# A down projection with four groups of block products done as seven products of sums

## The chip, the cores and the metric

The kernel runs on one core of one Trainium2 chip. Its engines work side by side and meet at semaphores: TensorE (PE in the profile, its weight loads PEld) multiplies, VectorE (DVE) and ScalarE (ACT) work element by element, GpSimd (POOL) does a few small steps, and SyncE (SP) issues nearly all transfers between HBM and on-chip memory (SBUF). TensorE writes to PSUM. The metric is the time of one execution in microseconds on the device, the median of several runs.

## What is computed

Two transformer blocks over 256 tokens of width 2048, in f32. The part that changes is the feed-forward step at the end of the first block:

```python
u = jnp.square(jax.nn.relu(jnp.einsum('bsd,df->bsf', h, w_up[l])))
x = x + rms_norm(jnp.einsum('bsf,fd->bsd', u, w_down[l]), norm_mlp_post[l])
```

`u` is 256 x 8192 and `w_down` 8192 x 2048. Ahead of it stand the first block's attention and the up projection, behind it the whole second block (its input projection `w_in_2` comes next) and the output.

## The kernel before

All large products run over a list of chunks. A chunk is 512 rows and up to 512 columns of a weight matrix, 1 MB; the program has 342, numbered in the order in which TensorE takes them. The down projection has chunks 176 to 239: four blocks of 512 output columns (`dn` 0 to 3), each 16 chunks deep. TensorE multiplies a chunk for both halves of the tokens (t = 0 and 1, 128 tokens each): per half 4 row tiles times 3 matmuls, so 24 matmuls of 128 x 512, summed in two banks of the PSUM tensor `acc`. The second PSUM tensor, `mis`, has four banks for side work.

Three matmuls take the place of one because every f32 operand is split into a high part and a rest, and high x high, high x rest and rest x high are added. The splits are the work around TensorE:

- A weight chunk is loaded by SyncE into one of `NRAW` = 3 buffers (`raw`, L398). ScalarE copies it into the high part (`high`, L578, tile `hi`), then VectorE subtracts (`low`, L994, tile `lo`). There are `NSPL` = 3 buffers for hi and lo, so the hi of a chunk waits for the product three chunks earlier; it is made two chunks ahead of its own product (`LEAD` = 2). A raw buffer is loaded again once the lo of its chunk is done.
- The operand from `u` is split the same way in pieces of 128 x 1024 (4 row tiles, both token halves) by `cut` (ScalarE L628, VectorE L1043), three chunks ahead, into one of four slots of `at`. Each of the four column blocks cuts all 16 pieces again, 64 cuts in all.

Each engine has its own queue and works it in order. A step n of the loops on ScalarE, VectorE and SyncE issues what belongs beside product n: the split of chunk n + 2, the cut for chunk n + 3, and side work named in a table (`beside`). `u` itself comes out of the up projection with tokens on partitions; it is turned block by block by VectorE and through HBM, one store and four loads for each of 16 pieces (`turned`); the last of these runs beside the first chunks of the down projection.

At the end of a column block ScalarE squares and copies the result out of PSUM (`evac`) to `Y2`; VectorE multiplies it with the norm's weights (`weigh`, steps 228 to 230 for the first three blocks). The change of stage to the next projection is written out by hand (`turnover`): TensorE does the first token half of the last three chunks, then the second half of two of them, so that the row mean, the norm and the transposes of the new rows for t = 0 run beside it; the first three chunks of the next stage are split early into `spare` buffers.

```python
def products(n, t):
    ...
    if n > 2:
        pe.wait_ge(s_lo, "lo", n)
    if source == "u":
        pe.wait_ge(s_dve, "cut", i)
    ...
        mm(o, a, hv[:, j, :], k + j == 0, False)
        mm(o, a, lv[:, j, :], False, False)
        r = mm(o, c, hv[:, j, :], False, k + j == nk - 1)
```

Of the kernel before, what the change touches and what calls it, by code (L numbers as in the profile page):

```python
# [15 lines left out]
P = 128  # L16
D = 2048
S = 256
# [3 lines left out]
NRAW = 3  # L22
# [4 lines left out]
N_W, N_AB, N_WO, N_UP, N_DN, N_IN2, N_RES, N_PG, N_ALL = 0, 80, 96, 112, 176, 240, 308, 326, 342  # L27
EARLY = {N_UP: (100, 101, 102), N_IN2: (231, 233, 237)}
# [41 lines left out]
def program(nc, x, xt, w_in, w_a, w_b, w_out, w_up, w_down, w_in2, w_out2, w_pg, w_pe, p2,  # L70
            cols, lamv, rpb, rows, bif, cos_c, sin_c, nam_c, id_c, lvl_c, caus_c, out):
    with ExitStack() as ctx:
# [82 lines left out]
        Y2 = t2(64, 2048)  # L155
        JK2 = SM[:, 0:512]
# [60 lines left out]
        for j in range(16):  # L217
            plan("up", j, w_up, 0, 16, 512 * j, 512, "r1")
        for j in range(4):
            plan("dn", j, w_down, 0, 64, 512 * j, 512, "u")  # L220
# [17 lines left out]
        on_dve = ("rope", "a", "b", "wo", "z", "g", "res")  # L238
# [5 lines left out]
        def freed(b):  # L244

            kind, j = blocks[b][:2]
            return s_dve if kind in on_dve or (kind, j) == ("dn", 3) else s_act
# [13 lines left out]
        nth = {c: i for i, c in enumerate(order)}  # L261
# [17 lines left out]

        side = {}  # L280
# [5 lines left out]
        turns_of.update({("hf", 0): 244, ("hf", 1): 248, ("qk", 0): 252, ("qk", 1): 256, ("hq", 0): 264, ("hq", 1): 268})  # L286
# [21 lines left out]
        for j in range(2):
            beside(272 + 4 * j, "turn_v", j)
        beside(266, "hg", 0, 0)  # L310
        for i, n in enumerate((268, 269, 271)):
            beside(n, "gate", i)
        for i in range(1, 13):
            beside(270 + i, "hg", 0, i)
        for i in range(13):
            beside(283 + i, "hg", 1, i)
        beside(295, "ml_logs", 0)
        for h in range(6):
            beside(296 + h, "ml", h)
        for g in range(2):  # L320
            beside(302, "ya", g)
        beside(316, "p_parts")
# [66 lines left out]
        def sync(e):  # L389
# [5 lines left out]
            def raw(n):  # L395
                if nth[n] >= NRAW:
                    sp.wait_ge(s_lo, "lo", order[nth[n] - NRAW])
                e.dma_start(raw_of(n).rearrange("p (k c) -> p k c", c=chunks[n][0].shape[-1]), chunks[n][0]).then_inc(  # L398
                    s_raw[nth[n] % NRAW].on("raw", n), 16)

# [23 lines left out]
            for n in order[8:]:  # L424
# [63 lines left out]
                if n == 231:  # L488
                    sp.wait_ge(s_dve, "cut", 49)
                    load(NB, rows[0:1, 2048:4096].squeeze(0).partition_broadcast(P), "nb2")  # L490
                if n == 260:
                    sp.wait_ge(s_dve, "cut", 63)
                    load(REV, id_c[1], "turn")
                if n == 309:
# [3 lines left out]
                if n == 313:  # L498
# [3 lines left out]
                raw(n)  # L502
# [7 lines left out]
        def gpsimd(e):  # L510
# [15 lines left out]
            for n in range(N_ALL):  # L526
# [17 lines left out]
                if n in (N_WO + 15, N_DN + 63):  # L544
# [6 lines left out]
                if n == 274:  # L551
# [9 lines left out]
        def scalar(e):  # L561
# [8 lines left out]
            def high(n):  # L570
# [4 lines left out]
                if N_IN2 <= n < N_IN2 + 3:  # L575
                    ac.wait_ge(s_dve, "cut", (53, 57, 63)[n - N_IN2])
# [46 lines left out]
            def cut(i):  # L623
                if i >= 64:
                    return
                ac.wait_ge(loaded("heads", ("ut", i % 16)), "heads", ("ut", i % 16))
                ac.wait_ge(s_prod, "products", N_DN + i - 4, 1)
                e.activation(ATH[:, 4 * (i % 4):4 * (i % 4) + 4, :], UT[:, 4 * (i % 16):4 * (i % 16) + 4, :], ACT.Copy).then_inc(  # L628
                    s_ach.on("cut hi", i))
# [140 lines left out]
            def square(b, t):  # L770
                ac.wait_ge(s_prod, "products", blocks[b][3][-1], t)
# [1183 lines left out]
```

## Time and profile before

| | |
|---|---|
| median of 3 runs | 1935.83 us (1935.59 to 1936.46) |
| profiled execution, first to last instruction | 1933.5 us |
| TensorE busy | 1922.0 us, 99% |
| VectorE busy | 1250.8 us, 65% |
| ScalarE busy | 983.0 us, 51% |
| transfers | 415 MB, 215 GB/s on average |

The profile shows one execution. "Busy" is the time in which an engine had an instruction at work; matmuls overlap, so their single durations add up to more than the busy time. In lists of groups, `out<-in` names the tiles; a matmul `acc<-hi,at` multiplies the high part of weights with the activations in `at`. An arrow `<-` in brackets names what ended the idle time before an instruction. A line number is that of the kernel's text, often that of a helper: L1589 is every matmul, L976 every `tensor_tensor` issued through `tt`.

### The profile page before, as it was taken

How to read it: one execution, taken by the hardware profiler on the slowest of the kernel's cores; microseconds unless marked ns; L12 is line 12 of the kernel's file. 1: busy time of each engine (PE TensorE's matmuls, PEld its weight loads, DVE VectorE, ACT ScalarE, POOL GpSimd, SP SyncE). 2: the span in 40 equal slices, each digit the busy share in tenths (PEclk: the TensorE clock that was granted, in tenths of full speed). 3: DMA queues.
4: the chain of work that ended last, by engine and by line, in shares of the span. 5: the costliest groups of instructions: out<-in, count | busy, mean ns of one | idle time of the engine just before them, and what ended most of it. 6: DMA issues, size and time to landing. Idle time of an engine off the chain costs nothing.

```text
span 1933.5 us, 21919 instructions
## 1 busy us (share of the span) xinstructions
PE 1922.0 (99%) x8770; PEld 1601.5 (83%) x8770; DVE 1250.8 (65%) x1255; ACT 983.0 (51%) x951; POOL 17.8 (1%) x31
## 2 busy tenths in 40 slices
PE   9999999999999999999999999999999999999998
PEld 7888888888888888888888888888889888888886
DVE  7747658845666644445466666677587869676655
ACT  6334445646445444444455555555555546544543
POOL 0000000000000000000000000000000000000000
PEclk9999999999999999999999999999999999999999
DMA  9876977765777388888886555565687544556753
GB/s 323 251 231 174 267 257 216 233 246 196 241 228 255 112 241 246 239 240 243 244 248 204 192 191 189 193 231 181 188 222 253 185 164 156 176 174 224 231 203 109
DMA packets 386151, 415.48 MB, mean 215 GB/s; under 512 B 192509, under 2 KB 205057, under 8 KB 385409
## 3 DMA queue, kind: packets, MB, share of 16 engines
q1 hardware_dynamic: 385032, 412.49, 68.6%
q10 hardware_dynamic: 1016, 1.59, 0.2%
q8 instruction: 69, 1.13, 0.2%
q14 instruction: 34, 0.27, 0.0%
HBM read 388.86 MB, written 25.17 MB: 214 GB/s over the span
## 4 chain that ended last, share of the span: by engine, by line
PE 95%; DVE 2%; ACT 1%; issue 1%; POOL 0%; POOLq 0%; DVEq 0%; ACTq 0%
PE acc L1589 92%; PE mis L1589 3%; ACT hi L578 1%; DVE lo L994 1%; DVE m L976 1%; PE mis L1592 1%; ACT m L567 0%; DVE m L984 0%; DVE at L1036 0%; ACT at L617 0%; DVE m L1294 0%; ACT xs L567 0%; DVE xs L976 0%; DVE sm L984 0%; POOLq L1892 0%
## 5 line engine op out<-in xcount | busy, mean ns | idle before, releaser
L1589 PE MATMUL acc<-hi,at 128*128 128x512 f32 (+1 forms) x5344 | 1650.6, 388 | 0.3 <-DVE lo L994 0.3
L1589 PEld LDWEIGHTS acc<-hi,at 128*128 128x128 f32 x5344 | 1000.4, 188 | 201.7 <-DVE lo L994 1.2
L994 DVE TENSOR_TENSOR lo<-raw,hi 128x2048 fp32r<-128x2048 f32 (+1 forms) x333 | 752.9, 2264 | 529.6 <-ACT hi L578 529.3
L1589 PE MATMUL acc<-lo,at 128*128 128x512 f32 (+1 forms) x2672 | 1032.5, 387 | 0.0
L578 ACT ACTIVATE hi<-raw 128x2048 fp32r<-128x2048 f32 (+1 forms) x333 | 628.4, 1891 | 522.0 <-PE acc L1589 476.7
L1589 PEld LDWEIGHTS acc<-lo,at 128*128 128x128 f32 x2672 | 501.8, 188 | 98.6
L567 ACT ACTIVATE m<-acc,st 128x512 f32<-128x512 f32 (+2 forms) x104 | 69.6, 669 | 86.3 <-PE acc L1589 85.2
L976 DVE TENSOR_TENSOR m<-m 128x256 f32<-128x256 f32 (+1 forms) x145 | 75.1, 518 | 20.9 <-ACT m L567 16.4
L567 ACT ACTIVATE m<-m 128x512 f32<-128x512 f32 (+4 forms) x71 | 58.2, 819 | 53.2 <-DVE m L976 37.9
L1043 DVE TENSOR_TENSOR at<-m,at 128x1024 fp32r<-128x1024 f32 x64 | 78.0, 1219 | 2.8 <-ACT at L628 2.8
L628 ACT ACTIVATE at<-m 128x1024 fp32r<-128x1024 f32 x64 | 66.6, 1041 | 7.5 <-PE acc L1589 7.5
L617 ACT ACTIVATE at<-m 128x512 fp32r<-128x512 f32 x40 | 25.1, 631 | 65.3 <-DVE m L976 51.1
L1589 PE MATMUL mis<-m 128*128 128x128 f32 (+3 forms) x316 | 53.0, 312 | 0.4 <-DVE m L976 0.4
L1589 PEld LDWEIGHTS mis<-m 128*128 128x128 f32 x316 | 45.7, 190 | 7.5 <-DVE m L976 1.7
L1126 DVE STREAM_TRANSPOSE m<-m 128x512 f32<-128x512 f32 x50 | 35.5, 709 | 2.9
L1036 DVE TENSOR_TENSOR at<-m,at 128x512 fp32r<-128x512 f32 x40 | 27.4, 688 | 13.0 <-ACT at L617 12.6
L1589 PE MATMUL acc<-spare,at 128*128 128x512 f32 x144 | 34.7, 394 | 0.0
L1589 PEld LDWEIGHTS acc<-spare,at 128*128 128x128 f32 x144 | 26.6, 188 | 5.4
L516 POOL TENSOR_TENSOR st<-st,mhalf 128x1 f32<-128x1 f32 (+3 forms) x20 | 14.9, 746 | 1703.1 <-DVE st L980 1617.9
L567 ACT ACT_TABLE_LOAD x20 | 25.7, 1283 | 3.2 <-issue 2.6
L568 ACT ACTIVATE m<-m,st 128x256 f32<-128x256 f32 x16 | 8.2, 510 | 37.1 <-DVE st L980 37.1
L568 ACT ACTIVATE sm<-xs 128x512 f32<-128x512 f32 (+1 forms) x18 | 10.5, 585 | 25.3 <-DVE xs L976 25.2
(134 smaller groups left out, 529.9 us busy)
## 6 DMA issues: line engine op xcount, KB each, us to landing
raw<-in_w_in SPq DMA_DIRECT2D x133, 1024.0 KB, 5.3
raw<-in_w_up SPq DMA_DIRECT2D x64, 1024.0 KB, 6.4
raw<-in_w_down SPq DMA_DIRECT2D x64, 1024.0 KB, 5.1
raw<-in_w_out SPq DMA_DIRECT2D x32, 1024.0 KB, 5.2
m<-turned SPq DMA_DIRECT2D x144, 128.0 KB, 4.6
raw<-in_w_pg SPq DMA_DIRECT2D x16, 1024.0 KB, 5.2
turned<-m SPq DMA_DIRECT2D x28, 512.0 KB, 6.0
raw<-in_w_in SPq DMA_DIRECT2D x12, 688.0 KB, 5.1
```

The lines of the kernel that those rows point to most:

```text
L567: return e.activation(o, i, f, scale=scale, bias=bias)
L568: return e.activation(o, i, f, scale=scale, bias=bias, accum_out=accum)
L578: e.activation(hi_of(n), raw_of(n), ACT.Copy).then_inc(s_hi.on("hi", n))
L617: e.activation(h, src, ACT.Copy).then_inc(s_ach.on("ath", name, g, t))
L628: e.activation(ATH[:, 4 * (i % 4):4 * (i % 4) + 4, :], UT[:, 4 * (i % 16):4 * (i % 16) + 4, :], ACT.Copy).then_inc(s_ach.on("cut hi", i))
L976: return e.tensor_tensor(o, a, b, op)
L994: e.tensor_tensor(lo, raw, hi.bitcast(F32), ALU.subtract).then_inc(s_lo.on("lo", n))
L1036: e.tensor_tensor(l, src, h.bitcast(F32), ALU.subtract).then_inc(s_dve.on("atl", name, g, t))
L1043: e.tensor_tensor(ATL[:, s4:s4 + 4, :], UT[:, k:k + 4, :], ATH[:, s4:s4 + 4, :].bitcast(F32), ALU.subtract).then_inc(s_dve.on("cut", i))
L1126: e.transpose(turned_to(j, t), src).then_inc(s_dve.on("turned", j, t))
L1589: return e.matmul(o, a, b, start=start, stop=stop)
L1592: return e.transpose(o, a, IDN[:, :])
```

## The change

Four groups of four chunks of the down projection are computed in another way. A group is 256 tokens x 1024 rows of `u` times 1024 x 1024 of `w_down`, cut into 2 x 2 blocks each: eight block products of 128 x 512 x 512. In their place come seven products of sums of blocks (Strassen's scheme in Winograd's order of sums). The column blocks are taken in two passes of 1024 columns; in each pass the `u` pieces 0 to 3 make two groups, A and B, and the pieces 4 to 15 stay ordinary chunks, `6a` being piece 6 times the pass's first 512 columns. A seven chunk, `A0` to `B6`, has 12 matmuls. The order of the 76 chunks is a table that alternates the two kinds.

What the seven chunks need: the block B11 of `w_down` is loaded into half of `Y2`, B12 into the other half (in the second pass, a free part of `u`), and VectorE adds in place: T1 = B11 + B12, T2 = T1 + B22, T3 = B12 + B22, T4 = T2 + B21 (`sums`). B22 and B21 come through the raw buffers, as chunks A3 and A5. On the side of `u`, VectorE makes four sums of 128 x 512 per group (`form`). Each seven chunk has its own split of weights and its own narrow cut of 128 x 512. Products 0, 1, 2 and 4 are summed over both groups in the four banks of `mis`; 3, 5 and 6 go straight to `acc`. At the end of a pass ScalarE copies one bank and VectorE mixes the others (`mixed`, four operations) into `Y2`, and the column blocks are added to these on VectorE when they leave PSUM. Before the turnover VectorE makes the last block in a tile `C22` (`mix_last`).

There are four raw buffers in place of three. An ordinary piece is cut once for both columns where its two chunks stand close. `weigh` moves to steps 6 to 4 ahead of the next stage.

```diff
-NRAW = 3
+NRAW = 4
+DN_ORDER = ("6a 6b 7a 7b 4a 4b A0 5a A1 5b A2 8a A3 8b A4 9a A5 9b A6 10a B0 10b B1 11a B2 12a B3 13a B4 14a B5 11b B6 12b 15a 13b 14b 15b".split(),
+            "6a 6b 7a 7b A0 4a A1 4b A2 5a A3 5b A4 8a A5 8b A6 9a B0 9b B1 10a B2 10b B3 11a B4 12a B5 13a B6 14a 15a 11b 12b 13b 14b 15b".split())
...
+        for c in order:
+            if not is_seven(c):
+                ring.append(c)
+            else:
+                p, g, q = chunks[c][6]
+                if q in (1, 4):
+                    ring.append(dn_at[p, "AB"[g] + str({1: 3, 4: 5}[q])])
...
             def raw(n):
                 if nth[n] >= NRAW:
-                    sp.wait_ge(s_lo, "lo", order[nth[n] - NRAW])
+                    past = ring[nth[n] - NRAW]
+                    sp.wait_ge(s_lo, "lo", past)
+                    if is_seven(past) and chunks[past][6][2] == 3:
+                        sp.wait_ge(s_dve, "sum", chunks[past][6][:2], "T3")
...
+            def sums(n):
+
+                p, g, q = chunks[n][6]
+                x, y = SUMS_OF[p][g], SUMS_OF[p][1 - g]
...
+                dv.wait_ge(s_lo, "lo", n)
+                if q == 0:
+                    dv.wait_ge(loaded("b12", p, g), "b12", p, g)
+                    tt(x, x, y, ALU.add).then_inc(s_dve.on("sum", (p, g), "T1"))
...
+                if q == 3:
+                    tt(y, y, as2(raw_of(b22)), ALU.add).then_inc(s_dve.on("sum", (p, g), "T3"))
...
+            def mixed(p):
...
+                tt(c21, p6, c11, ALU.add).then_inc(s_dve.on())
+                tt(c12, p5, c21, ALU.add).then_inc(s_dve.on())
+                tt(c21, p7, c21, ALU.add).then_inc(s_dve.on())
+                tt(c22, p7, c12, ALU.add).then_inc(s_dve.on("mixed", p))
...
+            def mix_last(t):
+                b = number["dn", 3]
+                dv.wait_ge(s_prod, "products", N_IN2 - 1, t)
+                tt(C22[:, t, :], acc[:, 2 * (b % 2) + t, :], mix_of(1, t, 1), ALU.subtract).then_inc(s_dve.on("evac", b, t))
...
+                    if kind == "dn" and j < 3:
+                        o = Y2[:, t, cols_]
+                        dv.wait_ge(s_prod, "products", ids[-1], t)
+                        tt(o, ps[t], o, ALU.subtract if j == 1 else ALU.add).then_inc(s_dve.on("evac", b, t))
...
+            def seven(n):
+
+                p, g, q = chunks[n][6]
...
+                pe.wait_ge(s_lo, "lo", n)
+                pe.wait_ge(s_dve, "cut", i)
+                for j in range(4):
+                    mm(o, ah[:, j, :], hv[:, j, :], opens and j == 0, False)
+                    mm(o, ah[:, j, :], lv[:, j, :], False, False)
+                    r = mm(o, al[:, j, :], hv[:, j, :], False, closes and j == 3)
```

The queues change at two places that matter below. SyncE, in the middle of the first pass. Before, every row is one chunk's load, and each waits for a lo (`s_weights_lo`):

```order
L398 DMA raw1<-in_w_down 128x4x512 [waits s_weights_lo]
L398 DMA raw2<-in_w_down 128x4x512 [waits s_weights_lo]
L398 DMA raw0<-in_w_down 128x4x512 [waits s_weights_lo]
L398 DMA raw1<-in_w_down 128x4x512 [waits s_weights_lo]
L398 DMA raw2<-in_w_down 128x4x512 [waits s_weights_lo]
```

Now, from the load of B12 of group A (two halves of 512 KB, `m<-in_w_down`) to that of B11 of group B; L502 are the blocks B22 (chunk A3) and B21 (chunk A5):

```order
L484 DMA m<-in_w_down 128x2x512 x2
L502 DMA raw3<-in_w_down 128x4x512 [waits s_weights_lo]
L496 DMA raw0<-in_w_down 128x4x512 [waits s_weights_lo]
L496 DMA raw1<-in_w_down 128x4x512 [waits s_weights_lo]
L496 DMA raw2<-in_w_down 128x4x512 [waits s_weights_lo]
L502 DMA raw3<-in_w_down 128x4x512 [waits s_dve_side,s_weights_lo]
L496 DMA raw0<-in_w_down 128x4x512
L496 DMA raw1<-in_w_down 128x4x512
L496 DMA raw2<-in_w_down 128x4x512 [waits s_weights_lo]
L484 DMA m<-in_w_down 128x2x512 [waits s_weights_lo]
```

The load of chunk A5 now waits for a sum too (`s_dve_side`), and those of 9a and 9b stand behind it without a wait of their own.

VectorE, at the end of the stage. Before, from the lo of the fifth chunk from the end (`lo1<-raw2`) to that of the last (`lo2<-raw1`, ahead of the last `spare`), then the turnover:

```order
L994 TENSOR_TENSOR lo1<-raw2,hi1 128x2048 [waits s_products,s_weights_hi]
L1043 TENSOR_TENSOR at<-m,at 128x4x256 [waits s_act_high]
L994 TENSOR_TENSOR spare32_56<-raw0,spare24_55 128x2048 [waits s_weights_hi]
L994 TENSOR_TENSOR lo2<-raw1,hi2 128x2048 [waits s_products,s_weights_hi]
L1043 TENSOR_TENSOR at<-m,at 128x4x256 [waits s_act_high]
L994 TENSOR_TENSOR lo0<-raw2,hi0 128x2048 [waits s_products,s_weights_hi]
L1043 TENSOR_TENSOR at<-m,at 128x4x256 [waits s_act_high]
L994 TENSOR_TENSOR lo1<-raw0,hi1 128x2048 [waits s_products,s_weights_hi]
L1043 TENSOR_TENSOR at<-m,at 128x4x256 [waits s_act_high]
L994 TENSOR_TENSOR lo2<-raw1,hi2 128x2048 [waits s_products,s_weights_hi]
L994 TENSOR_TENSOR spare56_59<-raw2,spare48_58 128x2048 [waits s_weights_hi]
L1383 TENSOR_REDUCE st<-st 128x1 [waits s_dve_side,s_act_side]
```

Now, from the four operations of `mixed` (`m<-mis,m`) to the first `mix_last` (`c22<-acc,m`). The lo of 12b, 13b, 14b and 15b are `lo2`, `lo0`, `lo1`, `lo2`:

```order
L1135 TENSOR_TENSOR m<-mis,m 128x512 [waits s_dve_side] x3
L1155 TENSOR_TENSOR spare32_56<-raw1,spare24_55 128x2048 [waits s_weights_hi]
L1155 TENSOR_TENSOR lo2<-raw2,hi2 128x2048 [waits s_products,s_weights_hi]
L1201 TENSOR_TENSOR at<-m,at 128x4x256 [waits s_act_high]
L1135 TENSOR_TENSOR m<-acc,m 128x512 [waits s_dve_side,s_products] x2
...
L1155 TENSOR_TENSOR lo0<-raw3,hi0 128x2048 [waits s_weights_hi]
L1201 TENSOR_TENSOR at<-m,at 128x4x256 [waits s_act_high]
L1135 TENSOR_TENSOR m<-m 128x512 [waits s_dve_side] x2
L1155 TENSOR_TENSOR lo1<-raw0,hi1 128x2048 [waits s_products,s_weights_hi]
...
L1155 TENSOR_TENSOR lo2<-raw1,hi2 128x2048 [waits s_products,s_weights_hi]
L1155 TENSOR_TENSOR spare56_59<-raw2,spare48_58 128x2048 [waits s_weights_hi]
L1135 TENSOR_TENSOR c22<-acc,m 128x512 [waits s_dve_side,s_products]
```

Between the lo of the last chunks stand now `mixed`, the evacuations (`m<-acc,m`), the three `weigh` (`m<-m`, two operations each) and, behind them, `mix_last`.

## Rows read from the trace of the kernel before

**Rows 1.** The page: its first line, and the start of the busy times.
```profile
span 1933.5 us, 21919 instructions
...
PE 1922.0 (99%) x8770; PEld 1601.5 (83%) x8770; DVE 1250.8 (65%) x1255; ACT 983.0 (51%) x951; POOL 17.8 (1%) x31
```

**Rows 2.** Waits of PE, whole span: us in total, times, longest us.
```profile
PE acc L1589 <- DVE lo L994: 0.3, 1, 0.3
```

**Rows 3.** Windows: length, busy us (instructions) of each engine, granted clock, DMA share, GB/s.
```profile
994.80:1342.90 348.10, 348.10 (x1543) 288.42 (x1542) 229.45 (x145) 194.00 (x151) 0.54 (x1) 1.00 0.62 207
1400.00:1800.00 400.00, 399.30 (x1972) 339.81 (x1971) 303.95 (x389) 210.99 (x215) 6.56 (x5) 1.00 0.62 196
1925.00:1933.50 8.50, 0.00 (x0) 0.00 (x0) 3.23 (x7) 2.28 (x7) 0.55 (x1) 0.67 0.34 124
```

**Rows 4.** Timeline of ACT, then DVE, steady part: start us, duration us, instruction.
```profile
1016.52 1.92 ACT L578 ACTIVATE hi<-raw 128x2048 fp32r<-128x2048 f32 x1 [2.58 <-PE acc L1589]
...
1021.96 1.92 ACT L578 ACTIVATE hi<-raw 128x2048 fp32r<-128x2048 f32 x1 [2.58 <-PE acc L1589]
...
1018.47 2.29 DVE L994 TENSOR_TENSOR lo<-raw,hi 128x2048 fp32r<-128x2048 f32 x1 [2.01 <-ACT hi L578]
1020.68 1.22 DVE L1043 TENSOR_TENSOR at<-m,at 128x1024 fp32r<-128x1024 f32 x1
```

**Rows 5.** Groups of DVE by shape: count, busy us, mean ns, idle us before.
```profile
L1036 DVE TENSOR_TENSOR at<-m,at 128x512 fp32r<-128x512 f32 x40 | 27.4, 688 | 13.0 <-ACT at L617 12.6
...
L976 DVE TENSOR_TENSOR xs<-xs 128x1024 f32<-128x1024 f32 x3 | 3.7, 1219 | 0.0
...
L976 DVE TENSOR_TENSOR m<-m 128x2048 f32<-128x2048 f32 x1 | 2.3, 2291 | 1.6 <-ACT m L567 1.6
```

**Rows 6.** Loads: landing times, all of `w_down`; a pair of `w_in`; SyncE's issues.
```profile
L398 SPq DMA_DIRECT2D raw<-in_w_down x64: 367/368/989, 974.3 to 1314.6; - x64
...
DMA to landing us min/median/max: 4.9/5.1/6.8
...
raw<-in_w_in SPq DMA_DIRECT2D x1, 1024.0 KB, 6.0
...
raw<-in_w_in SPq DMA_DIRECT2D x1, 1024.0 KB, 7.1
...
66.25 2.00 SPq L398 DMA_DIRECT2D raw<-in_w_in  x2
...
1010.82 6.44 SPq L393 DMA_DIRECT2D m<-turned  x4
```

**Rows 7.** Timeline of DVE at the end of the stage and in the turnover.
```profile
1288.57 1.49 DVE L976 TENSOR_TENSOR m<-m 128x512 f32<-128x512 f32 x2
...
1309.00 1.22 DVE L1043 TENSOR_TENSOR at<-m,at 128x1024 fp32r<-128x1024 f32 x1
1310.13 2.29 DVE L994 TENSOR_TENSOR spare<-raw,spare 128x2048 fp32r<-128x2048 f32 x1
...
1328.55 2.29 DVE L994 TENSOR_TENSOR lo<-raw,hi 128x2048 fp32r<-128x2048 f32 x1 [2.01 <-ACT hi L578]
1330.76 2.29 DVE L994 TENSOR_TENSOR spare<-raw,spare 128x2048 fp32r<-128x2048 f32 x1
...
1345.01 0.16 DVE L1383 TENSOR_REDUCE st<-st 128x1 f32<-128x4 f32 x1
...
1350.62 2.28 DVE L994 TENSOR_TENSOR lo<-raw,hi 128x2048 fp32r<-128x2048 f32 x1
```

**Rows 8.** Timeline of ACT and PE in the turnover.
```profile
1334.76 0.60 ACT L568 ACTIVATE sm<-acc 128x512 f32<-128x512 f32 x1 [4.44 <-PE acc L1589]
1335.25 0.19 ACT L568 ACTIVATION_READ_ACCUMULATOR sm<-acc 128x1 f32 x1
...
1353.97 0.48 PE L1589 MATMUL acc<-hi,at 128*128 128x512 f32 x1
```

More of the change, by code:

```diff
@@ L265, in raw_of @@
         def raw_of(n):
+            if is_seven(n) and n not in nth:
+                p, g, q = chunks[n][6]
+                return SUMS_OF[p][g if q != 4 else 1 - g]
             return RAW[nth[n] % NRAW][:, 0:4 * chunks[n][1]]
@@ new lines, in program, with part_of @@
+        assert [operands[operand_of[N_IN2 - 4 + g]][4] for g in range(4)] == [0, 1, 2, 3], last_use
+        cuts_at, forms_at = {}, {}
+        for i, o in enumerate(operands):
+            cuts_at.setdefault(o[7] - 3, []).append(i)
+            if o[0] == "form" and o[3] in (1, 2, 3, 4):
+                forms_at.setdefault(o[7] - 5, []).append(i)
+        form_raw = {i for z in forms_at.values() for i in z}
+        def part_of(z, i):
+            kind, a, b, c, slot, h = operands[i][:6]
+            tok = slice(0, S) if kind == "k" else slice(h * P, h * P + P)
+            return z[:, 4 * slot:4 * slot + 4, tok]
@@ L501, in sync @@
                     load(PTT, p2.rearrange("p (k s) -> p k s", k=2), "p")
-                raw(n)
+                if is_seven(n):
+                    seven(n)
+                else:
+                    raw(n)
             for t in range(2):
@@ L623, in cut @@
             def cut(i):
[L624 to L629, printed above, removed]
+                if operands[i][6] is not None:
+                    ac.wait_ge(s_prod, "products", operands[i][6], 1)
+                if i in form_raw:
+                    ac.wait_ge(s_dve, "form", i)
+                else:
+                    for k in kept_in(i):
+                        ac.wait_ge(loaded("heads", ("ut", k)), "heads", ("ut", k))
+                e.activation(part_of(ATH, i), value_of(i), ACT.Copy).then_inc(s_ach.on("cut hi", i))
             def lam():
@@ L965, in scalar @@
                 beside_products(n)
+                for p in range(2):
+                    if n == dn_at[p, "B6"]:
+                        ac.wait_ge(s_lo, "lo", n)
+                        ac.wait_ge(s_prod, "products", dn_at[p, "B0"], 1)
+                        act(mix_of(p, 0, 0), mis[:, place.get(("shared", p, 0), 0), :], ACT.Copy).then_inc(s_act.on("shared", p))
         def vector(e):
@@ L990, in low @@
                 hi, lo, raw = hi_of(n), lo_of(n), raw_of(n)
+                if is_seven(n):
+                    hi, lo, raw = as2(hi), as2(lo), raw if n not in nth else as2(raw)
                 dv.wait_ge(s_hi, "hi", n)
@@ L1551, in vector @@
                         low(c)
-                if N_DN <= n < N_IN2:
-                    cut(n - N_DN + 3)
+                        if is_seven(c):
+                            sums(c)
+                for i in cuts_at.get(n, ()):
+                    cut(i)
+                for i in forms_at.get(n, ()):
+                    form(i)
+                for p in range(2):
+                    if n == dn_at[p, "B6"] + 1:
+                        mixed(p)
                 for c in ahead.get(n, ()):
@@ L1667, in products, with seven @@
                 r.then_inc(s_prod.on("products", n, t))
+            def seven(n):
+                p, g, q = chunks[n][6]
+                hv, lv = (cut4(z(n)) for z in (hi_of, lo_of))
+                i = operand_of[n]
+                ah, al = part_of(ATH, i), part_of(ATL, i)
+                if q in (0, 1, 2, 4):
+                    if g == 0:
+                        take(("shared", p, q), s_dve, "mixed", p)
+                    o = mis[:, place["shared", p, q], :]
+                else:
+                    o = acc[:, {3: 2, 5: 0, 6: 1}[q], :]
+                opens, closes = q in (0, 1, 2, 4) and g == 0, q in (0, 1, 2, 4) and g == 1
+                pe.wait_ge(s_lo, "lo", n)
[4 more added lines that the diff above has]
+                    r = mm(o, al[:, j, :], hv[:, j, :], False, closes and j == 3)
+                r.then_inc(s_prod.on("products", n, 1))
             def first():
```

246 lines of the change are left out of this document (194 added, 52 removed).

## Prediction

> **What bounds the kernel now.** I read the page's head first. TensorE is busy 1922.0 of 1933.5 us [rows 1]: 11.5 us are left, and the list of what TensorE waited for has one entry on the split weights, 0.3 us [rows 2]. Then the windows: the whole down projection has no gap (348.10 of 348.10 us), at granted clock 1.00, while VectorE is busy 229.45 and ScalarE 194.00 us of it; of the idle 11.5 us, 8.5 are the end of the program, behind the last product [rows 3]. So a TensorE instruction removed is worth its whole pitch, as long as the split (ScalarE hi, then VectorE lo) keeps its lead. The steady rows give both numbers: ScalarE's hi starts when the product three chunks back ends, every 5.44 us, so one matmul of 24 costs 5.44/24 = 0.2267 us, and hi, lo, cut take VectorE 2.29 + 1.22 us of each 5.44 [rows 4].
>
> The profiled span stands 2.3 us under the median 1935.83; I carry all differences to the median.
>
> **What is removed.** A group of four chunks (8 block products of 12 matmuls) becomes seven chunks of 12. Four groups save 4 x 12 = 48 matmuls of 128x512: 48 x 0.2267 = **10.9 us**. Each matmul keeps its own weight load, its 512 moving columns and the same types, so I keep the pitch for the products that go to `mis`. Nothing else on TensorE changes.
>
> **What is added to VectorE.** 12 more splits, 16 sums of 128x2048, 16 forms of 128x512, 8 for `mixed`, 8 evacuations that ScalarE did or that are new; 30 fewer wide cuts, 28 more narrow ones. The prices are all in rows: a plain 128x2048 sum in f32 took 2.29 us, like a split's lo, the in-place sum of half that size 1.22, a narrow cut 0.69 [rows 5]. In a full queue an instruction takes less: lo to the next start 2.21 us, a wide cut 1.13, two dependent 128x512 operations 1.49, so 0.80 each [rows 7]. By the same overlap I take 0.60 for a narrow cut and 0.72 for a form; a sum waits for its lo to end, so 2.32.
>
> *Inside a group.* From A0 to 10a TensorE has 7 x 2.72 + 7 x 5.44 = 57.1 us. VectorE has 14 lo (30.9), 4 sums (9.3), 4 wide cuts (4.6), 7 narrow ones (4.2), 4 forms (2.9): 51.9. In the B group of the first pass there are 7 wide cuts: 54.0. So 91 to 95% of TensorE's time: it keeps up, nearly without reserve. A split's lead shrinks from 10.88 to 8.16 us (a seven chunk and an ordinary one), and hi plus lo need 4.2.
>
> *The loads inside a group.* Here a wait is added. SyncE sends the raw block of A5 only when the sum T3 has read the buffer of A3, and two ordinary loads (9a first) are queued behind it. Count from the end of 5b: hi of A3 1.92, lo 2.29, T3 2.32, so 6.5. A 1 MB load lands 5.1 us after its issue (median of 64); of two loads issued 1.63 us apart (2.00 for both issues less 0.37 for one) the second landed 2.7 us behind the first (66.25 + 6.0 = 72.25, 67.88 + 7.1 = 74.98) [rows 6]. So 9a lands at 6.5 + 5.1 + 2.7 = 14.3, is split at 14.3 + 0.1 + 1.92 + 2.29 = 18.6. TensorE reaches it after A2, 8a, A3, 8b, A4, at 19.04. The margin is 0.4 us, four times (9a, 14a, 8a, 12a). Between the bounds zero (all margins hold) and 2.3 each (three loads that share the engines evenly: the last at 5.1 + 2 x 2.7 = 10.5, so 2.7 later, less the margin) I take 0.1 each, near the lower one, since the row shows loads landing in turn: **0.5 us**.
>
> The Trainium skill (DMA: Bandwidth & Descriptors, section "Anatomy of one DMA — SWDGE (gpsimd) path") prices a load at 2.0 us plus its bytes at 436 GB/s. An estimate by that page: 4.4 us for 1 MB and 6.8 for the second of a pair, so a margin of 1.4 us and no stall; the measured 5.1 decides here. Without the page everything else stands.
>
> *The first group* also has B12 behind the last turned store. Before, the four turned loads were issued from 1010.82 until 1017.3 [rows 6]; B12 follows, lands near 1022.9, while T1 could start at 1020.8 (hi of A0 at 1016.52 [rows 4], plus 4.2). VectorE is held 2 us and ends the lo of 5a at 1028.6 (T1 2.3, a wide cut 1.1, lo 2.3); TensorE comes to it after 4a, 4b and A0, at 1016.52 + 2 x 5.44 + 2.72 = 1030.1. Hidden by 1.5 us.
>
> *The end of the second pass.* Here the queue gets longer than its cover. Count from the end of product 12a, when ScalarE may start the hi of B6 (1.92). VectorE then has, with no gap: lo and cut for B6 (3.35); lo, cut, a spare lo for 14a (5.55); lo and cut for 15a (3.35); lo, cut, four `mixed` at 0.80, a spare lo for 11b (8.75); lo and cut for 12b, two evacuations (4.95). That is 27.9 us. ScalarE is behind the second evacuation with its square (0.68 with the accumulator [rows 8]) and only then makes the hi of 13b: 2.6, in place of VectorE's `weigh` of 1.6. Then lo, cut and `weigh` for 13b and for 14b, 4.95 each, and the lo of 15b, 2.29: 42.7. TensorE runs B5, 13a, B6, 14a, 15a, 11b, 12b in 2 x 2.72 + 5 x 5.44 = 32.6, and the turnover asks for 14b after 2.72 and 15b after 5.44 more, at 38.1. So 14b comes some 2.3 us late and 15b 2.3 more: **4.6 us**. Before, the lo of that last chunk ended at 1330.84 [rows 7] and TensorE came at 1332.0 (its half product ended at 1334.76 [rows 8]): the `weigh` steps stood six chunks earlier and neither `mixed` nor the evacuations were there. Bounds: 3.5 if the queue packs as tightly as the tightest row, 7 if each of its 25 instructions loses 0.1 us to a wait.
>
> *The turnover.* `mix_last` puts one 128x512 (0.72) ahead of each square. For t = 0 the first transposes wait for TensorE anyway. For t = 1 the reduce started at 1345.01, behind a full queue [rows 7]; now the copy to C22 starts there, and its square follows: 1.4 us later, so the lo at 1350.62 ends at 1354.3, where TensorE wanted it at 1353.97 [rows 8]: **0.4 us**.
>
> *The fourth raw buffer* lets every load elsewhere start earlier or as before; TensorE waited for none, so nothing (0.5 us either way, through the order of the first loads).
>
> **Sum.** 1935.8 - 10.9 + 0.5 + 4.6 + 0.4 = **1930.4 us**; the span would be 1928.1.
>
> **Rivals.** (1) *The whole saving arrives*: the end is covered, since VectorE runs ahead more than my count has it, or the margins are wider; stalls under 2 us. 1935.8 - 10.9 + 0 to 2.5 = 1925 to 1927.5. For it: inside the groups the count leaves reserve. Against it: the last stretch is a sum of priced rows. Chance 0.20. (2) *More waits than the count*: 0.1 us lost at each of the 25 instructions of the end (2.5) and 1 us at each load margin (4): 1936.9, no measurable change. Chance 0.14. (3) *The loads share the engines* rather than landing in turn: 4 x 2.3 in place of 0.5, 1939.1, within 0.2% too. Against it stands the pair of rows 6. Chance 0.04. (4) *VectorE becomes the bound in all four groups*, on the slower side: a sum in place, over two halves of 1024, costs more than my 2.3 us. It decides from 2.3 + (57.1 - 54.0)/4 = 3.1 us on; at twice the price, 4.6, each group lacks 51.9 + 9.3 - 57.1 = 4.1 to 6.2 us, some 20 in all, and the end starts later still: about 1951. The in-place row (1.22 us for 1024) speaks against it. Chance 0.06. (5) *TensorE's clock falls at the stalls.* The granted clock was 1.00 (2.4 GHz) through a stretch with 0.70 us of idle, and 0.67 as a mean over the final 8.5 us, where TensorE had nothing to do: there it fell to its lower level, 1.2 GHz [rows 3]. If the 2.3 us waits at 14b and 15b did that too, the two half products there (5.4 us) would take twice as long: 1935.8, no change. Chance 0.02. The Trainium skill (TensorE: Matmul & The Clock Gate, section "HAM oscillation — how this bites in real kernels") describes that: waits between groups of matmuls return the clock to half rate. The fall in the last row agrees; whether waits this short do it no run here shows.
>
> **Chances and range.** The forecast has 0.54. About 0.2% (3.9 us) is what a measurement of this kernel can tell from no change. Faster by more, below 1932.0: the forecast nearly whole (0.52) and (1): 0.72. Within: (2), (3), (5): 0.20 with what is left of the forecast. Slower: (4) with the tail of (3): 0.08. The range 1925.5 to 1935.0 leaves out (4), (3), the upper half of (2) and the edge of (1).
>
> **What would show it.** 48 matmuls fewer at 0.227 us each; lo of 14b and 15b releasing TensorE, some 2 us each, at the end of the stage; one short wait at the ordinary chunk behind each A4 or B4, on a lo whose hi waited for a load; a sum at 2.3 us. It would be wrong if VectorE has idle time between the lo of B6 and that of 15b, if the sums cost over 3 us, or if the matmuls into `mis` have another pitch.

## The result, and the profile after

The changed kernel takes 1939.2 us (median of 13 executions, 1937.9 to 1940.9) beside 1935.5 for the kernel before: ratio 1.0018, 95% interval 1.0010 to 1.0026. The 3.7 us are within the 0.2% that I had called no change, though the interval leaves out 1; they are 8.8 us above the forecast of 1930.4 and outside its range. All 48 matmuls are gone, as the page of the changed kernel shows (the profiled execution is the slowest of the thirteen, 1940.9):

```profile
span 1938.1 us, 21956 instructions
...
PE 1916.9 (99%) x8722; PEld 1594.7 (82%) x8722; DVE 1317.1 (68%) x1313; ACT 987.6 (51%) x957; POOL 18.8 (1%) x31
```

Against [rows 1] that is 48 matmuls fewer, but only 5.1 us less busy time where 10.9 were due, and a span 4.6 us longer. The list of TensorE's waits (us in total, times, the longest), which had 0.3 us on the split weights [rows 2], now has

```profile
PE acc L1816 <- DVE lo L1155: 9.6, 7, 3.7
```

One of the seven, 0.26 us far behind in the second block, is the wait of [rows 2]. The other six one by one, from the timeline of TensorE (start us, duration, instruction, idle time before it and what ended it). They are the first matmuls of 8a and 12a in the second pass, of 13b, 14b and 15b, and of a chunk in the turnover:

```profile
1222.74 0.50 PE L1816 MATMUL acc<-hi,at 128*128 128x512 f32 x1 [1.16 <-DVE lo L1155]
1223.08 0.40 PE L1816 MATMUL acc<-lo,at 128*128 128x512 f32 x1
...
1283.88 0.80 PE L1816 MATMUL acc<-hi,at 128*128 128x512 f32 x1 [3.70 <-DVE lo L1155]
...
1324.00 0.50 PE L1816 MATMUL acc<-hi,at 128*128 128x512 f32 x1 [0.18 <-DVE lo L1155]
...
1328.79 0.50 PE L1816 MATMUL acc<-hi,at 128*128 128x512 f32 x1 [1.78 <-DVE lo L1155]
...
1333.72 0.50 PE L1816 MATMUL acc<-hi,at 128*128 128x512 f32 x1 [1.92 <-DVE lo L1155]
...
1358.50 0.50 PE L1816 MATMUL acc<-hi,at 128*128 128x512 f32 x1 [0.66 <-DVE lo L1155]
```

Together 9.4 us. The last is the matmul that stood at 1353.97 [rows 8]: 4.5 of the 4.6 us lie ahead of it. The windows (length, busy us and instructions of each engine, granted clock, DMA share, GB/s) show no idle time in the first pass (the first row holds all of it), and where the missing busy time went: behind the waits at 12a and 15b TensorE ran at its lower level, 0.50 of full speed.

```profile
977.00:1183.00 206.00, 206.00 (x909) 170.13 (x908) 168.88 (x110) 117.61 (x94) 0.00 (x0) 1.00 0.64 219
...
1276.00:1280.00 4.00, 4.00 (x19) 3.13 (x17) 1.35 (x2) 0.41 (x1) 0.00 (x0) 1.00 1.05 388
1284.00:1287.00 3.00, 3.00 (x7) 2.35 (x8) 2.96 (x3) 3.00 (x3) 0.00 (x0) 0.50 0.01 3
1335.10:1338.40 3.30, 3.30 (x10) 2.53 (x9) 1.01 (x2) 0.00 (x0) 0.00 (x0) 0.50 0.95 346
```

What such a stretch costs can be read from 12a. It starts at 1283.88, and ScalarE's next hi, which waits for its last product, starts at 1291.22 (a row shown further down): 7.34 us in place of 24 x 0.2267 = 5.44, and 0.1 for the step from engine to engine: 1.8 us. Two stretches are 3.6.

The sum of this execution: -10.9 + 9.4 of waits + 3.6 of clock + 0.7 of a late start (the second group of products began at 7.82 us, before at 7.06) = +2.8. Most of the other 1.8 us stands beside the waits. From start to start, the matmul that waited comes 0.1 to 0.2 later than its idle time says, and at the waits that fall at full clock the next one comes 0.11 late as well (1222.74 to 1223.08 is 0.34 in place of 0.23): some 1.5 us for six waits. In the first pass the first two matmuls of 9a come 0.27 late in the same way, without a listed wait.

**Why 12a came late.** ScalarE's hi of the ordinary chunk behind A4 or B4, in the four groups in turn (9a, 14a, 8a, 12a), and with them the hi of B6, from ScalarE's timeline:

```profile
1059.16 1.92 ACT L726 ACTIVATE hi<-raw 128x2048 fp32r<-128x2048 f32 x1 [3.67 <-DMA raw<-in_w_down]
...
1116.33 1.92 ACT L726 ACTIVATE hi<-raw 128x2048 fp32r<-128x2048 f32 x1 [3.40 <-DMA raw<-in_w_down]
...
1218.45 1.92 ACT L726 ACTIVATE hi<-raw 128x2048 fp32r<-128x2048 f32 x1 [4.83 <-DMA raw<-in_w_down]
...
1279.59 1.91 ACT L726 ACTIVATE hi<-raw 128x2048 fp32r<-128x2048 f32 x1 [7.38 <-DMA raw<-in_w_down]
...
1291.22 1.92 ACT L723 ACTIVATE hi<-m 128x2048 fp32r<-128x2048 f32 x1 [4.13 <-PE acc L1816]
```

All four wait for a load. T3, the sum that lets the loads go, from VectorE's timeline (the first and the last of the four):

```profile
1048.75 2.29 DVE L1135 TENSOR_TENSOR m<-m,raw 128x2048 f32<-128x2048 f32 x1
...
1265.45 2.29 DVE L1135 TENSOR_TENSOR m<-m,raw 128x2048 f32<-128x2048 f32 x1
```

From the end of T3 to the hi it is 8.1 and 7.9 us in the first pass, where the prediction had 7.9, and TensorE does not wait. In the second pass it is 9.3 and 11.85. SyncE's issues around the last T3 (1267.74) show why:

```profile
1245.50 0.37 SPq L496 DMA_DIRECT2D raw<-in_w_down  x1
1267.83 0.37 SPq L502 DMA_DIRECT2D raw<-in_w_down  x1
1268.24 0.52 SPq L484 DMA_DIRECT2D m<-in_rows  x1
1268.79 2.68 SPq L496 DMA_DIRECT2D raw<-in_w_down  x3
```

The queue stands still for 22 us, and then five loads of 1 MB go out in 3.6 us. Between B5's block (L502) and 12a's (first of L496) stands a load that the prediction did not count: the weight row of the next norm, 1 MB over all partitions (L484, `nb2` in the code), which the step table puts at 12a's place. So 12a is third of the burst, not second. The landings of 9a and of 12a (KB, us from issue):

```profile
raw<-in_w_down SPq DMA_DIRECT2D x1, 1024.0 KB, 7.6
...
raw<-in_w_down SPq DMA_DIRECT2D x1, 1024.0 KB, 10.7
```

The Trainium skill (DMA: Bandwidth & Descriptors, section "Anatomy of one DMA — SWDGE (gpsimd) path") gives 2.0 us plus the bytes at 436 GB/s, for loads that GpSimd issues; these are SyncE's. By that page three loads in turn would be there 9.2 us after the first issue, an estimate. The trace has the third 11.7 us after it (1268.79 + 10.7 - 1267.83), and the measurement decides.

**The end of the second pass** went as counted: the queue of VectorE from the hi of B6 (1291.22) to the end of the lo of 15b (1333.67) is 42.5 us, where the prediction had 42.7, and the waits there are 3.9 in place of 4.6. VectorE's lo of 15b:

```profile
1331.38 2.29 DVE L1155 TENSOR_TENSOR lo<-raw,hi 128x2048 fp32r<-128x2048 f32 x1
```

### The profile page after: what moved, and what is told of

It is laid out like the page before. It is cut to its first block, busy times and chain, and to the rows that moved or that the text cites. A ratio compares the mean times of both kernels' runs of the same rounds, so it can differ in the third digit from the quotient of the medians.

```text
span 1938.1 us, 21956 instructions
## 1 busy us (share of the span) xinstructions
PE 1916.9 (99%) x8722; PEld 1594.7 (82%) x8722; DVE 1317.1 (68%) x1313; ACT 987.6 (51%) x957; POOL 18.8 (1%) x31
## 4 chain that ended last, share of the span: by engine, by line
PE 90%; DVE 5%; ACT 2%; issue 2%; DMA 1%; POOL 0%; SPq 0%; POOLq 0%; DVEq 0%; ACTq 0%
PE acc L1816 85%; PE mis L1816 5%; DVE lo L1155 2%; DVE m L1135 1%; ACT hi L726 1%; DMA raw<-in_w_down 1%; PE mis L1819 0%; DVE at L1201 0%; DVE xs L1143 0%; DVE spare L1155 0%; DVE at L1197 0%; ACT hi L723 0%; DMA raw<-in_w_in 0%; ACT m L702 0%; DVE m L1143 0%
## 5 line engine op out<-in xcount | busy, mean ns | idle before, releaser
L1816 PE MATMUL acc<-hi,at 128*128 128x512 f32 (+1 forms) x5184 | 1608.4, 389 | 9.9 <-DVE lo L1155 9.6
L1816 PEld LDWEIGHTS acc<-hi,at 128*128 128x128 f32 x5184 | 971.9, 188 | 208.6 <-DVE lo L1155 13.5
L1816 PE MATMUL acc<-lo,at 128*128 128x512 f32 (+1 forms) x2592 | 1002.5, 387 | 0.0
L726 ACT ACTIVATE hi<-raw 128x2048 fp32r<-128x2048 f32 (+1 forms) x317 | 597.5, 1889 | 436.0 <-PE acc L1816 380.8
L1135 DVE TENSOR_TENSOR m<-m 128x256 f32<-128x256 f32 (+2 forms) x149 | 84.2, 565 | 21.3 <-ACT m L702 16.3
L723 ACT ACTIVATE hi<-m 128x2048 fp32r<-128x2048 f32 x20 | 38.4, 1919 | 58.4 <-PE acc L1816 58.4
L1155 DVE TENSOR_TENSOR lo<-m,hi 128x2048 fp32r<-128x2048 f32 x20 | 45.8, 2291 | 15.2 <-ACT hi L723 15.2
L1201 DVE TENSOR_TENSOR at<-m,at 128x1024 fp32r<-128x1024 f32 (+1 forms) x46 | 49.7, 1081 | 2.2 <-ACT at L779 1.9
L779 ACT ACTIVATE at<-m 128x1024 fp32r<-128x1024 f32 (+1 forms) x46 | 42.8, 930 | 3.5 <-PE acc L1816 3.5
L1816 PE MATMUL mis<-hi,at 128*128 128x512 f32 x128 | 42.0, 389 | 0.0
```

What stands on the lines that cost most here:

```text
L723: e.activation(as2(hi_of(n)), raw, ACT.Copy).then_inc(s_hi.on("hi", n))
L726: e.activation(hi_of(n), raw_of(n), ACT.Copy).then_inc(s_hi.on("hi", n))
L779: e.activation(part_of(ATH, i), value_of(i), ACT.Copy).then_inc(s_ach.on("cut hi", i))
L1135: return e.tensor_tensor(o, a, b, op)
L1155: e.tensor_tensor(lo, raw, hi.bitcast(F32), ALU.subtract).then_inc(s_lo.on("lo", n))
L1201: e.tensor_tensor(part_of(ATL, i), value_of(i), part_of(ATH, i).bitcast(F32), ALU.subtract).then_inc(s_dve.on("cut", i))
```

## The experiments

Times are medians; the ratio is to the kernel before, measured beside it. "Squares later" holds "both"; the two rows under it add one edit each to it, and "all" adds the two together.

| kernel | us | before | ratio, 95% interval |
|---|---|---|---|
| row load early | 1933.89 | 1935.33 | 0.9990 (0.9981 to 0.9999) |
| weigh early | 1935.34 | 1935.33 | 1.0000 (0.9992 to 1.0009) |
| both | 1931.90 | 1935.33 | 0.9981 (0.9972 to 0.9990) |
| before, four raw buffers | 1935.85 | 1935.33 | 1.0002 (0.9993 to 1.0010) |
| squares later | 1929.09 | 1935.70 | 0.9967 (0.9955 to 0.9979) |
| squares later + lo in the turnover | 1928.87 | 1935.70 | 0.9965 (0.9953 to 0.9978) |
| squares later + load first | 1926.86 | 1935.70 | 0.9956 (0.9943 to 0.9968) |
| all | 1926.58 | 1935.70 | 0.9955 (0.9942 to 0.9967) |

**1. The row load one step earlier.** Its own wait (the last use of the memory it writes) is over long before.

```diff
-                if n == N_IN2 - 11:
+                if n == N_IN2 - 12:
                     sp.wait_ge(s_dve, "cut", operand_of[dn_at[1, "A6"]])
                     load(NB, ..., "nb2")
```

> One edit: the load of the weight row (nb2, 1 MB) is issued one step earlier, ahead of the load of B5's raw block that waits for the sum T3, so that it no longer stands between that load and the one of 12a. Theory A (the row load makes 12a land third in place of second): 12a, which landed 10.7 us after its issue and 11.85 us after the end of T3 (8.1 and 7.9 in the first pass), comes some 2.5 to 3 us earlier; the 3.7 us stall falls to 0.5 to 1.5, the granted clock stays at 1.00 there, and the half rate stretch of 3.4 us, worth 1.7, goes: about 4.2 less than the changed kernel, 1935.0. Rival B (VectorE's queue in the group is late, T3 with it): the order of the loads does not matter, the stall stays near 3.7, 1939. Rival C (the clock falls for another reason than the stall): the stall goes but the stretch at half rate stays, 1936.7.

1933.89, 5.3 less than the changed kernel. SyncE and, last row, ScalarE's hi of 12a:

```profile
1245.72 0.51 SPq L484 DMA_DIRECT2D m<-in_rows  x1
1267.64 0.37 SPq L502 DMA_DIRECT2D raw<-in_w_down  x1
1268.06 3.24 SPq L496 DMA_DIRECT2D raw<-in_w_down  x3
```
```profile
1275.39 1.92 ACT L726 ACTIVATE hi<-raw 128x2048 fp32r<-128x2048 f32 x1 [3.37 <-DMA raw<-in_w_down]
```

The row load goes out in the idle 22 us, 12a is second of the burst, lands after 7.3 us, and its hi starts 7.8 us after the end of T3 (1267.56), as in the first pass. The wait at 12a is gone altogether, more than I expected, and from 1280 to 1332 the granted clock is 1.00. Theory A holds; B and C fall. The waits at 14b and 15b stay (the longest 1.9).

**2. The weigh steps out of the last chunks** (row load as in the changed kernel).

```diff
-            beside(N_IN2 - 6 + i, "weigh", i)
+            beside((N_IN2 - 11, N_IN2 - 11, N_IN2 - 3)[i], "weigh", i)
```

The last three steps of a stage belong to the turnover, so the third weigh was not issued at all: this kernel and the next leave out the weighting of the third column block, two operations, 1.42 us.

> One edit: the three weigh steps (two 128x512 products with the weight row each, 1.42 us) leave the last six chunks of the second pass: two go behind the split of 13a, ahead of the hi of B6, where VectorE sat idle 2.5 us; the third behind the split of 15b. Theory A (the queue of VectorE from the lo of B6 on, 42.5 us without a gap, makes 14b and 15b late): 4.3 us leave the queue, the stalls at 13b, 14b and 15b (0.2 + 1.8 + 1.9) go but for 0.5, the clock stays at 1.00 at the end: 5 less than the changed kernel, 1934. Rival B (ScalarE's hi of 13b behind the square is what is late): 14b keeps a stall of 1 us, 15b none: 1936. Rival C (loads of the last chunks are late): no change, 1939.

1935.34, 3.9 less than the changed kernel. The three waits at 13b, 14b and 15b shrank from 3.9 to 0.55, 0.32 and 0.28, and the clock stayed at 1.00 there:

```profile
1324.30 0.50 PE L1816 MATMUL acc<-hi,at 128*128 128x512 f32 x1 [0.55 <-DVE lo L1155]
...
1327.64 0.50 PE L1816 MATMUL acc<-hi,at 128*128 128x512 f32 x1 [0.32 <-DVE lo L1155]
...
1330.97 0.50 PE L1816 MATMUL acc<-hi,at 128*128 128x512 f32 x1 [0.28 <-DVE lo L1155]
```

A is right that VectorE's queue made the end late, and C falls. 1.2 us stayed, where A had 0.5, and the time lies between A's 1934 and B's 1936; the omitted weigh is a part of the relief, and experiment 5 does it elsewhere.

**3. Both edits.**

> Both edits together: the weight row's load one step earlier, the weigh steps out of the last chunks. Theory A (two separate waits, each with its own stretch at half clock): the gains add, 4.2 + 5, about 1930, the stalls left being 8a in the second pass (1.2), up to 1 at 12a, and the turnover (0.7). Rival: when 12a comes in time TensorE reaches the end of the pass 4 us earlier and the queue of VectorE is that much more behind; the gain of the first edit is lost there: 1933 to 1935.

1931.90, 7.3 less than the changed kernel, where the single gains sum to 9.2. That is between theory A (about 1930) and its rival (from 1933 on): the gains do not simply add. There is one wait left at the end, 13b, and these rows of ScalarE, VectorE, TensorE and the windows tell whose it is:

```profile
1315.61 0.63 ACT L703 ACTIVATE sm<-m 128x512 f32<-128x512 f32 x1
1316.14 0.19 ACT L703 ACTIVATION_READ_ACCUMULATOR sm<-m 128x1 f32 x1
1316.24 1.90 ACT L726 ACTIVATE hi<-raw 128x2048 fp32r<-128x2048 f32 x1
```
```profile
1314.07 1.49 DVE L1135 TENSOR_TENSOR m<-acc,m 128x512 f32<-128x512 f32 x2
1318.17 2.29 DVE L1155 TENSOR_TENSOR lo<-raw,hi 128x2048 fp32r<-128x2048 f32 x1 [2.61 <-ACT hi L726]
```
```profile
1320.51 0.50 PE L1816 MATMUL acc<-hi,at 128*128 128x512 f32 x1 [1.90 <-DVE lo L1155]
```
```profile
1321.50:1324.50 3.00, 3.00 (x8) 2.35 (x8) 3.00 (x3) 2.13 (x2) 0.00 (x0) 0.50 0.96 311
```

VectorE, now early, stands idle for 2.6 us: it waits for the hi of 13b, which ScalarE makes only behind the squares (L703), and these wait for VectorE's evacuation (1314.07). Here a single wait of 1.90 us was followed by a stretch at half clock.

**4. The fourth raw buffer alone**, in the kernel before, with the smaller scratch area that makes room for it.

```diff
-NRAW = 3
+NRAW = 4
...
+    nc = _bacc.Bacc("TRN2", ..., dynamic_dma_scratch_size=512)
```

> The kernel before with only the fourth raw buffer and the smaller scratch area that pays for it. Theory A (the 0.74 us by which the changed kernel is behind from the first 10 us on comes from them): the first products start at 5.5 in place of 5.1 us, the offset stays to the end, 0.7 more than the kernel before: 1936.2. Rival B (the late start is chance, or comes from the other code): the start is the one of the kernel before, 1935.5. Rival C (the deeper prefetch hides something): under 1935.

1935.85 beside 1935.33: 0.5 more, and the interval holds no change. Its first products start at 5.24, the ones of the changed kernel at 5.55, the ones of the kernel before at 5.10. It cannot be told from the kernel before.

**5. The squares behind the hi of 13b**, on the kernel with both edits, the third weigh issued in the turnover.

```diff
+                if n == N_IN2 - 5:
+                    evac(number["dn", 2])
...
-                    if n < N_ALL - 1:
+                    if n == dn_at[1, "15a"]:
+                        pass
+                    elif n < N_ALL - 1:
                         evac(b)
...
                 if name == "r2":
+                    weigh(2)
                     mix_last(0)
```

> The row load early and the weigh steps early as in the kernel with both edits (there the weigh of the third column block was not issued at all, so that kernel left 1.4 us of VectorE's work and one weighting out; here it stands in the turnover, ahead of the last mix, and is done). New edit: ScalarE makes the squares of the third block's rows one chunk later, behind the hi of 13b. Theory A (with VectorE relieved, the 2.3 us wait at 13b is the hi of 13b standing behind the squares, which wait for VectorE's evacuation): hi of 13b starts 2.3 us earlier, right behind product 15a, the stall goes, and with it the stretch at half clock (1.7): 4 less than 1931.9, about 1928. Rival B (the hi waits for the raw block or for the product three chunks back as long): the stall stays above 1.5 us, 1931 to 1932. Rival C (VectorE is late at 14b and 15b all the same): the wait moves there, 1930.

1929.09, 2.8 less than with both edits, with more work done. VectorE's lo of 13b:

```profile
1313.25 1.49 DVE L1139 TENSOR_TENSOR m<-acc,m 128x512 f32<-128x512 f32 x2
1314.65 2.28 DVE L1159 TENSOR_TENSOR lo<-raw,hi 128x2048 fp32r<-128x2048 f32 x1
```

It follows the evacuation without a gap, the wait at 13b is gone, and one of 0.31 us at 14b is all that the end has left. Theory A. The wait in the turnover grew from 0.9 to 1.32: the third weigh stands in its queue now.

**6. The lo in the turnover earlier.**

```diff
                 if name == "r2":
                     mix_last(1)
+                    low(n0 + 3)
...
-                low(n0 + 3)
+                if name == "r1":
+                    low(n0 + 3)
```

> As the run with the squares later, and the lo of the chunk three behind the turn (ready since its hi, but late in VectorE's queue) is made right behind the last mix of t = 1, partly in the 0.8 us in which VectorE waits for the square. Theory A (the 0.9 us wait in the turnover is that lo's place in the queue): the wait goes, 0.9 less than the run with the squares later. Rival B (the chain of the second row is as tight: mean, weighting, row added, transposes): it ends 1.5 us later (2.3 less 0.8) and TensorE waits for it instead: 0.5 to 1.5 more.

1928.87 beside 1929.09: no difference that these runs can tell. The wait on the lo is gone, and TensorE waits at the second row's transposes instead, for the row that VectorE adds:

```profile
1343.10 1.44 PE L1826 MATMUL mis<-idn,xs 128*128 128x128 f32 x8 [0.89 <-DVE xs L1147]
```

Rival B: the chain of the second row was as tight as the lo.

**7. The ordinary block ahead of A5's raw block.**

```diff
-                if q in (1, 4):
-                    ring.append(dn_at[p, "AB"[g] + str({1: 3, 4: 5}[q])])
+                if q in (1, 5):
+                    ring.append(dn_at[p, "AB"[g] + str({1: 3, 5: 5}[q])])
...
-                        if is_seven(c):
+                        if is_seven(c) and chunks[c][6][2] != 4:
                             sums(c)
+                        if is_seven(c - 1) and chunks[c - 1][6][2] == 4:
+                            sums(c - 1)
```

(The raw load in SyncE's `seven` moves with it.)

> As the run with the squares later, and in each group the ordinary block behind A4 (B4) is loaded ahead of A5's (B5's) raw block: it takes the buffer that T3 frees, A5's takes the next; the sum T4 moves behind the lo of that ordinary chunk. Theory A (the load margin: the ordinary load lands second behind T3, 7.3 to 8.4 us after its issue; alone it lands in 5.0 to 5.8): hi of 9a, 14a, 8a, 12a starts 2 to 3 us earlier, the 1.3 us stall at 8a in the second pass goes: 1.3 less than the run with the squares later. Rival B (VectorE is the limit in the group: T3, lo of A4 and T4 stand in front whatever lands first): 8a stays within 0.3 of where it was. Rival C (T4 now comes later and A6's hi waits for it): the stall moves to A6, same time.

1926.86, 2.2 less than with the squares later. SyncE, then ScalarE's hi of 9a and 12a, then VectorE's lo of 9a and T4 behind it:

```profile
1050.37 0.37 SPq L496 DMA_DIRECT2D raw<-in_w_down  x1
1050.78 0.51 SPq L502 DMA_DIRECT2D raw<-in_w_down  x1
```
```profile
1055.53 1.92 ACT L726 ACTIVATE hi<-raw 128x2048 fp32r<-128x2048 f32 x1 [0.77 <-DMA raw<-in_w_down]
...
1270.39 1.92 ACT L726 ACTIVATE hi<-raw 128x2048 fp32r<-128x2048 f32 x1 [0.75 <-DMA raw<-in_w_down]
```
```profile
1057.48 2.29 DVE L1159 TENSOR_TENSOR lo<-raw,hi 128x2048 fp32r<-128x2048 f32 x1 [0.21 <-ACT hi L726]
1059.69 2.28 DVE L1139 TENSOR_TENSOR m<-m,raw 128x2048 f32<-128x2048 f32 x1
```

The hi now starts 5.2 us after the end of T3 in these two groups (1050.30 and 1265.17), and 5.4 and 5.8 after it at 14a and 8a: 2.5 to 3.5 earlier than with the squares later. The wait at 8a is gone, and none came at A6: theory A. Of the 2.2 us, by the starts of the matmuls, 8a accounts for 1.4, 9a for 0.3 and 12b for 0.2.

**8. All edits.**

> All edits: row load and weigh early, squares later, the lo in the turnover earlier, ordinary loads ahead of A5's and B5's raw. Theory A (the waits are independent): no wait over 0.5 us in the down projection or the turnover, the granted clock 1.00 until the end, and the time of before less the 48 products: 1935.3 - 10.9 = 1924.5 to 1926. Rival (each wait that goes uncovers one of like size): 1928 or more.

1926.58, 9.1 less than the kernel before, of the 10.9 that the products are worth, and not to be told from the 1926.86 of experiment 7. The page, the waits and a window that holds the whole down projection:

```profile
span 1924.4 us, 21956 instructions
...
PE 1911.4 (99%) x8722; PEld 1591.9 (83%) x8722; DVE 1316.7 (68%) x1313; ACT 988.3 (51%) x957; POOL 18.8 (1%) x31
```
```profile
PE mis L1828 <- DVE xs L1147: 0.9, 1, 0.9
PE acc L1825 <- DVE lo L1159: 0.6, 2, 0.3
```
```profile
977.00:1340.00 363.00, 362.40 (x1606) 299.55 (x1604) 313.84 (x219) 210.85 (x168) 2.10 (x2) 1.00 0.61 210
```

TensorE's busy time is 10.6 us under [rows 1]. The new waits come to 1.2 us, 0.28 at 14b and 0.90 at the second row's transposes in the turnover; the other 0.30 on a lo is again the wait of [rows 2]. VectorE is busy for 313.84 of 363 us, 86%, without holding anything up for over a microsecond. Theory A is nearly right: one wait is over its 0.5, and the time is 0.6 above its top.

**9. Two of the kernels again, for their traces.**

> The kernel with the row load early, once more, for its profile. Its 11 times lie from 1932.1 to 1935.0, and its profiled execution (1932.8) had the two waits at 14b and 15b (2.1 and 2.3 us between starts) and no stretch at half clock. Theory A (whether the clock falls after such waits changes from execution to execution, 3.4 us at half rate each time, so 1.7 us): the same two waits stand in the trace, with or without a fall; with one, the time is some 1.7 more than 1932.8, 1934.5. Rival B (the waits themselves vary): other waits, of other lengths.

> The changed kernel once more, for its profile. Theory A: the waits at 8a, 12a, 14b and 15b are there within 0.3 us (1.3, 3.9, 1.9, 2.1 between starts, each less one pitch); the late start of 0.74 us, which two of the seven kernels with the fourth raw buffer showed, is chance and may be missing; after the 3.9 us wait the granted clock falls again, at the end perhaps. Rival B: the start is late again and belongs to the changed kernel.

The kernel with the row load early had its two waits again and, again, the full clock (1931.97). Of its 11 times above, five lie from 1932.1 to 1932.8 with a mean granted clock of 0.998, and five from 1934.0 to 1935.0 with 0.997. The distance is about one stretch at half clock, which fits; no trace of one of the later five was taken.

The changed kernel (1938.76) had the same waits at the same places, the longest 3.6, and no late start: its first products began at 5.23, so the 0.7 us of the first trace are chance. Its clock fell differently, for longer at 12a and not at all at the end. There 12a took 8.6 us from its first matmul (1282.81) to ScalarE's next hi (1291.40), so this one fall cost 3.1 us in place of 1.8:

```profile
1283.00:1288.00 5.00, 5.00 (x12) 3.94 (x13) 4.96 (x4) 3.02 (x3) 0.00 (x0) 0.50 0.25 60
1332.00:1337.00 5.00, 3.10 (x13) 2.55 (x14) 4.07 (x3) 0.01 (x1) 0.00 (x0) 1.00 0.65 215
```

## Why the prediction was wrong, step by step

- *48 matmuls at 0.2267 us.* Right: the count, and 10.6 us of busy time once the waits and the half clock are gone (experiment 8).
- *Inside a group VectorE keeps up.* Right: a sum took 2.29 us, the lo of 12a came when its load came, and with the load in time VectorE held the four groups (experiments 1 and 7). One sum was off: by its own prices the B group of the first pass comes to 55.3 us, not 54.0 (three wide cuts more at 1.13); VectorE was busy for 54.3 of the 57.1 us of that group's products, and held it. Rival (4) is out. So is (3): of the burst behind the last T3 the first three loads landed one after the other, 5.0, 7.1 and 10.7 us after their issues. That its number, 1939.1, is nearly the measured 1939.2 is chance: it had equal waits at all four margins, and there were none listed at two of them.
- *The first group.* Right: no wait, and none listed in the whole first pass. T1 held VectorE for 0.6 us in place of 2.
- *The loads inside a group.* **This is the step that failed.** The count itself, 7.9 us from T3 to the hi, was right for the two groups of the first pass (8.1 and 7.9). But I wrote the margin of 0.4 "four times", as if the queue behind T3 were alike in all groups. In the last one the weight row's load stands in it. Before, that load had cost nothing at its place; behind a blocked queue it leaves in the same burst. It took 3.7 us of wait, beyond the bound of 2.3 that I had worked out for three loads sharing. At 8a the load went out 0.3 us later than in the first pass and landed after 8.4 us in place of 7.6 and 7.3, which with so thin a margin is the wait of 1.16. It is no chance, since the hi of 8a came 9.3 us after T3 in experiments 1 and 5 too; why it went out and landed later stays open. Past 7.9 and the margin of 0.4 the count gives waits of 1.0 and 3.5 for the 9.3 and 11.85 measured, so its arithmetic holds and its landing times do not. The term of 0.5 us measured 4.9.
- *The end of the second pass.* Right: mechanism and queue (42.5 for 42.7), waits of 3.9 for 4.6. I had also named the hi of 13b behind the squares; experiment 3 shows it as the next in line, at 1.9 us, when VectorE is relieved.
- *The turnover.* Mechanism right, size short: 0.66 to 0.9 for 0.4.
- *The fourth raw buffer.* Zero within what can be measured (experiment 4).
- *The clock.* Rival (5) happened, beside the forecast and not in place of it. I had given it 0.02 and a price for two whole half products at half rate, 5.4. It cost some 1.8 us for a stretch and came twice in the profiled execution, once and for 3.1 us in the other trace. It should have been a term tied to every wait in the sum, and stood there at nothing. The Trainium skill (TensorE: Matmul & The Clock Gate, section "HAM oscillation — how this bites in real kernels") describes waits that return the clock to half rate, of 3 to 5 us in its example. The trace now agrees behind a wait of 3.70; that the clock also fell behind a single one of 1.90 (experiment 3) and behind the pair of 1.78 and 1.92 goes beyond that example.

So 1930.4 + 4.4 (load margins) + about 3.5 (clock) + 0.3 (turnover) - 0.7 (end) comes to 1937.9, and the median is 1939.2; the remaining 1.3 is of the size of what the waits cost beyond their idle time. My rival (2), more waits, at 1936.9, had the right sign; it spread them over the four margins and the end, where one queue made most of it.

## What to carry to other kernels

When a change puts a wait into an in-order queue, list every transfer that the queue's table places behind that wait, group by group, and not the pattern of one group: what was free at its place leaves in the same burst as what is urgent. Loads without a near deadline belong ahead of the wait, and of the others the one with the nearest deadline first; here that was worth 5.3 and 2.2 us for edits of one line and of a few. Then add to each wait of TensorE the price of its clock, and expect behind the queue that you relieve the next engine's: VectorE's queue at the end hid ScalarE's hi behind the squares.

## What was not expected of the hardware

TensorE's granted clock fell to 0.50 behind waits of 3.6 to 3.7 us in each of the three traces that have one (the changed kernel's two, and experiment 2). Behind waits of 1.7 to 1.9 us it fell in two traces (the changed kernel's first, and both edits) and not in three others (the changed kernel's second, and both traces with the row load early), so with the same program it falls in one execution and not in another. In the first trace of the changed kernel a fall cost about 1.8 us, half as much as the longest wait; in the second, one fall cost 3.1. And of a burst of five 1 MB loads issued within 3.6 us the first landed after 5.0 us, the third after 10.7, the last after 13.7; meanwhile the DMA engines moved 388 GB/s (the window from 1276).
